# Cached key pages turned on VectorE instead of TensorE, and prompt scores issued one block ahead

## The reference

```python
# prompt, in query blocks of 128 (ci, cum_k: running sums of the log forget values)
s = jnp.einsum('bqhd,bkhd->bhqk', qi, k).astype(jnp.float32) * FOX_SCALE
s = s + jnp.swapaxes(ci, 1, 2)[..., :, None] - cum_k[:, :, None, :]
p = jax.nn.softmax(jnp.where(mask, s, MASK_VALUE), axis=-1)
o = jnp.einsum('bhqk,bkhd->bqhd', p.astype(v.dtype), v)
# samples: pages are taken from a pool by a table
k_past = cache_k[page_table].reshape(DB, P, FOX_HEADS, FOX_DH)
s = jnp.concatenate([jnp.einsum('bqhd,bkhd->bhqk', q, k_past),
                     jnp.einsum('bqhd,bkhd->bhqk', q, k_new)], axis=-1).astype(jnp.float32) * FOX_SCALE
s = s + jnp.swapaxes(cum_new, 1, 2)[..., :, None] - cum_k[:, :, None, :]
p = jax.nn.softmax(jnp.where(mask, s, MASK_VALUE), axis=-1)
o = jnp.einsum('bhqk,bkhd->bqhd', p[..., :P], v_past) + jnp.einsum('bhqk,bkhd->bqhd', p[..., P:], v_new)
```

## Time and profile before

| | us |
|---|---|
| three runs | 2152.65, 2160.13, 2160.87 |
| median | 2160.13 |
| profiled execution, device time | 2150.99 |
| its span | 2149.2 |

### The profile page before, as it was taken

One profiled execution on the slowest core, in us unless ns is written; L12 is line 12 of the kernel. 1 busy time (PEld: TensorE's weight loads), 2 busy tenths in 40 slices (PEclk: granted clock), 3 DMA queues, 4 the chain that ended last, 5 costly groups with the idle time before them and its releaser, 6 DMA issues.

```text
span 2149.2 us, 37580 instructions
## 1 busy us (share of the span) xinstructions
PE 2037.4 (95%) x16263; PEld 1893.7 (88%) x16263; DVE 900.7 (42%) x980; ACT 620.3 (29%) x794; POOL 577.6 (27%) x130
## 2 busy tenths in 40 slices
PE   4999999999889999999999999889998899999998
PEld 3979979979679999999999999666665899999998
DVE  3445245254447424333535325354453562424251
ACT  3222232231235111111233422444444331212121
POOL 1312412503314333333333222000000333333331
PEclk9999999999999999999999999999998899999999
DMA  5142441341423222222321224675763222322221
GB/s 148 63 154 92 138 159 38 128 167 40 142 104 98 79 79 79 78 81 88 100 69 59 79 79 144 228 257 173 246 224 105 93 79 80 96 81 78 78 84 58
DMA packets 169029, 238.87 MB, mean 111 GB/s; under 512 B 12930, under 2 KB 131842, under 8 KB 168706
## 3 DMA queue, kind: packets, MB, share of 16 engines
q1 hardware_dynamic: 151554, 212.61, 30.2%
q10 hardware_dynamic: 17264, 23.79, 3.1%
q0 software_dynamic: 80, 0.52, 0.1%
HBM read 210.77 MB, written 26.12 MB: 110 GB/s over the span
## 4 chain that ended last, share of the span: by engine, by line
PE 65%; issue 23%; DVE 4%; POOL 4%; ACT 2%; DMA 1%; SPq 0%; POOLq 0%; ACTq 0%; DVEq 0%
PE PS L741 15%; PE PS L740 15%; PE PS L742 15%; POOL w_lo L697 4%; PE PS L780 3%; PE PS L781 3%; PE PS L782 3%; PE PS L1167 2%; PE PS L1118 1%; PE PS L1129 1%; PE PS L1155 1%; DVE probs L2099 1%; PE PS L1110 1%; PE PS L1187 1%; PE PS L1228 1%
## 5 line engine op out<-in xcount | busy, mean ns | idle before, releaser
L697 POOL TENSOR_TENSOR w_lo<-w_raw,w_hi 128x2048 fp32r<-128x2048 f32 (+1 forms) x125 | 576.1, 4609 | 1540.4 <-ACT w_hi L1343 1540.4
L1343 ACT ACTIVATE w_hi<-w_raw 128x2048 fp32r<-128x2048 f32 (+1 forms) x125 | 237.9, 1903 | 1028.3 <-PE PS L742 839.6
L740 PE MATMUL PS<-x_hi,w_hi 128*128 128x296 f32 (+1 forms) x1664 | 498.4, 300 | 9.3 <-DVE x_lo L1758 6.1
L741 PE MATMUL PS<-x_lo,w_hi 128*128 128x296 f32 (+1 forms) x1664 | 498.0, 299 | 0.0
L742 PE MATMUL PS<-x_hi,w_lo 128*128 128x296 f32 (+1 forms) x1664 | 497.1, 299 | 0.0
L740 PEld LDWEIGHTS PS<-x_hi,w_hi 128*128 128x128 f32 x1664 | 314.9, 189 | 11.8 <-DVE x_lo L1758 7.5
L741 PEld LDWEIGHTS PS<-x_lo,w_hi 128*128 128x128 f32 x1664 | 314.8, 189 | 0.2
L742 PEld LDWEIGHTS PS<-x_hi,w_lo 128*128 128x128 f32 x1664 | 314.7, 189 | 0.0
L742 PE MATMUL PS<-hidden_hi,w_lo 128*128 128x296 f32 (+1 forms) x1024 | 304.9, 298 | 0.0
L741 PE MATMUL PS<-hidden_lo,w_hi 128*128 128x296 f32 (+1 forms) x1024 | 304.3, 297 | 0.0
L740 PE MATMUL PS<-hidden_hi,w_hi 128*128 128x296 f32 (+1 forms) x1024 | 304.3, 297 | 0.0
(11 more groups left out here) (237 smaller groups left out, 2614.7 us busy)
## 6 DMA issues: line engine op xcount, KB each, us to landing
w_raw<-in_w_mlp_up SPq DMA_DIRECT2D x32, 1024.0 KB, 5.4
w_raw<-in_w_mlp_down SPq DMA_DIRECT2D x32, 1024.0 KB, 5.2
k_page<-in_cache_k SPq DMA_DIRECT2D x64, 512.0 KB, 4.8
v_page<-in_cache_v SPq DMA_DIRECT2D x64, 512.0 KB, 5.4
w_raw<-in_w_ret_in SPq DMA_DIRECT2D x24, 1024.0 KB, 6.1
sample_state<-in_state_ret SPq DMA_DIRECT2D x32, 512.0 KB, 5.4
out_state_ret_sample<-sample_state ACTq DMA_DIRECT2D x32, 512.0 KB, 4.3
w_raw<-in_w_ret_out SPq DMA_DIRECT2D x16, 512.0 KB, 3.4
```

Source lines behind the costliest of these rows:

```text
L697: pool.tensor_tensor(lo, raw, hi.bitcast(F32), ALU.subtract).then_inc(lo_done, 1)
L740: pe.matmul(o, wh[:, w], xh[:, t, cols], start=(t == 0), stop=False)
L741: pe.matmul(o, wh[:, w], xl[:, t, cols], start=False, stop=False)
L1343: act.activation(part(WH[n.slot], n), part(WR[n.slot], n), ACT.Copy).then_inc(hi_done, 1)
```

## The change

- **Key pages.** SP fetches a page in four DMAs, one for each group of four heads, each onto 32 partitions: partition `32a + r` holds rows `r, 32 + r, 64 + r, 96 + r`, of each the 256 floats of heads `4a` to `4a + 3`. DVE turns the page with one transpose instruction, which transposes every 32x32 square within its 32 partitions, into one of four `k_page_t` tiles of eight groups `j`; partitions then hold four heads x 32 dimensions. There are no page turns on PE and no page copies on ACT and DVE any more.
- **Queries.** `q_blocks` is built once for all samples, block diagonal: 32 columns are four heads x 8 queries. The order of heads in sample scores, in `selb` and in the value products follows it.
- **Page scores** are made for two pages at once (`pair_scores`): eight products of 256 columns for a pair.
- **Prompt pairs.** `scores(j)` stands before `probs_t(j - 1)`, in other PSUM banks (3 to 5 for scores, 4 and 6 for turned probabilities, 7 for values); `scores` waits for the exponentials of `j - 1`. The normalising moves from DVE to ACT, and the two reciprocals become one instruction.
- **Metas.** The two heads' probabilities lie side by side in one tile, so the metas of a pair are turned as one 128x32 square, and multiplied by a block-diagonal `meta_v_by_head` in one product.
- **Sample probabilities** are turned into banks 6, 7 and 2; the second half waits for `gated` of the round's slot 0. `out_t` stands first in its slot.
- **Buffers.** Four key and six value buffers; the first two weight blocks of the output projection are loaded at the end of the stage.

The diff, cut to its core:

```diff
-NKS, NVS = 5, 5
+NKS, NVS = 4, 6
+NTURN = 4
...
             def k_page(kn):
+
                 if kn < NPAGE * DB:
-                    page_in(PT1, kn, k_pool, KR, NKS, k_in)
+                    rows = io["cache_k"][page_at(kn)].rearrange("o (i r) (a h) d -> a r (o i) (h d)", r=32, a=4)
+                    for a in range(4):
+                        sp.dma_start(KR[kn % NKS][32 * a:32 * a + 32, :].rearrange("r (i f) -> r i f", i=4), rows[a]) \
+                            .then_inc(k_in[kn % NKS], 16)
...
             for b in range(DB + 1):
...
+                for p in range(4):
+                    k_next(b, p)
+                for p in range(4, 8):
+                    if b == DB and p == 4:
+                        sp.wait_ge(ss_ready, DB)
+                        weights(Blk(N_OUT), w_fo[:, :, 0:BW])
+                    k_next(b, p)
+                    v_next(b - 1, 2 * p - 8)
+                    v_next(b - 1, 2 * p - 7)
+            weights(Blk(N_OUT + 1), w_fo[:, :, BW:2 * BW])
...
                 if j:
-                    pe.wait_ge(pt_evac, 3 * j)
+                    pe.wait_ge(ex_done, 2 * j)
...
                 if j:
                     pe.wait_ge(pv_evac, j)
-                for par in range(2):
-                    src = PP[par][:, m:m + NMETA] if par == 0 else PP[par][:, 0:NMETA]
-                    last = pe.transpose(PS[0:NMETA, 6, 2 * P + P * par:3 * P + P * par], src, ident)
-                last.then_inc(pt_ready, 1)
+                pe.transpose(PS[0:2 * NMETA, 7, 2 * P:3 * P], PP[:, NKEY - NMETA:NKEY + NMETA], ident) \
+                    .then_inc(pt_ready, 1)
...
+            def pair_scores(b, r):
+
+                n = 4 * b + r
+                pe.wait_ge(k_turned, 2 * n + 2)
+                if n == 0:
+                    pe.wait_ge(qb_done, 1)
+                s = 2 * n % NTURN
+                q_k(b, r // 2, slice(2 * P * (r % 2), 2 * P * (r % 2) + 2 * P), lambda j: KP[:, s:s + 2, j, :]) \
+                    .then_inc(sc_used, 1)
...
                 pe.wait_ge(sex_done, b + 1)
...
+                for half, ready in enumerate((sp0_ready, sp1_ready)):
+                    if half:
+                        pe.wait_ge(pv_evac, 4 * b + 3)
                     for p in range(4):
...
+            def slot0(b, j):
+                if b > 1:
+                    out_t(b - 2)
+                if live(j):
+                    scores(j)
+                    probs_t(j - 1)
+                if b > 0:
+                    pair_scores(b - 1, 3)
+                    new_scores(b - 1)
+                if live(j):
+                    values(j - 1)
+
+            def slot1(b, j):
+                if live(j):
+                    probs_t(j - 1)
+                    scores(j)
+                    values(j - 1)
+                if b < DB:
+                    bias(b)
+                if b > 0:
+                    probs_t_s(b - 1)
+                if 0 < b < DB:
+                    pair_scores(b, 0)
...
+            def normed_probs(j):
+                act.wait_ge(inv_row, j + 1)
+                n = keys_of(j % 4)
+                for par in range(2):
+                    x = own_probs(par, n)
+                    act.activation(x, x, ACT.Copy, scale=RM[:, par:par + 1]).then_inc(pn_done, 1)
...
+            def turn_page(kn):
+
+                dve.wait_ge(k_in[kn % NKS], 64 * (kn // NKS + 1))
+                if kn >= NTURN:
+                    dve.wait_ge(sc_used, (kn - NTURN) // 2 + 1)
+                dve.transpose(KP[:, kn % NTURN], KR[kn % NKS][:].rearrange("p (i j c) -> p j i c", i=4, j=8)) \
+                    .then_inc(k_turned, 1)
...
+                    if live(j):
+                        for par in range(2):
+                            maximum(j, par)
+                    if k:
+                        turn_page(NPAGE * b + 2 * i)
+                    if live(j):
+                        inverse_sums(j)
                     if i == 0 and v:
                         maxima_s(b - 1)
+                    if k:
+                        turn_page(NPAGE * b + 2 * i + 1)
+                    if live(j - 1):
+                        gated(j - 1)
                     if i == 1 and v:
                         probs_copy_s(b - 1)
...
+                    if i == 3 and v:
+                        output_s(b - 1)
             gated_s(DB - 1)
```

More of the change, by code:

```diff
@@ L1112, in scores, with query @@
[L1112 to L1121 removed]
+                def query(par):
+                    rows = slice(DH * par, DH * par + DH)
+                    return rows, TQ[rows, 1 + qb, P * t:P * t + P]
@@ new lines, in scores @@
+                if qb == 3:
+                    pe.wait_ge(pt_evac, 3 * j - 2)
+                for par in range(2):
+                    pe.matmul(parts(par)[1], sel(par), CU[:, 0:NMETA], start=(par == 0 and qb == 3), stop=False,
+                              skip_group_check=True)
+                for par in range(2):
+                    rows, q = query(par)
+                    if par == 1 and qb == 3:
+                        pe.wait_ge(s_ready, 2 * j + 1)
+                    pe.matmul(parts(par)[1], q, KTT[rows, t, NSAMP:W0], start=False, stop=True, skip_group_check=True)                         .then_inc(s_ready, 1)
@@ L1306, in _, with slot3 @@
+            def slot3(b, j):
+                if live(j):
+                    scores(j)
+                    probs_t(j - 1)
+                    pair_scores(b, 2)
+                if b > 0:
+                    page_values(b - 1, 4)
+                    page_values(b - 1, 5)
+                if live(j):
+                    values(j - 1)
+                if b > 0:
+                    page_values(b - 1, 6)
+                    page_values(b - 1, 7)
+                    new_values(b - 1)
             pe.wait_ge(rounded, 1)
@@ L1307, in _ @@
             for b in range(DB + 1):
[L1308 to L1317 removed]
+                slot0(b, pair_at(b, 0))
+                slot1(b, pair_at(b, 1))
+                slot2(b, pair_at(b, 2))
@@ L1713, in _ @@
+                    if live(j - 1):
+                        probs_copy(j - 1)
+                    if live(j):
+                        for par in range(2):
+                            exp(j, par)
+                        normed_probs(j)
+                    if i == 0 and b > 0:
+                        exp_s(b - 1)
+                    if i == 1 and b > 0:
+                        probs_copy_s(b - 1)
+            w_hi(Blk(N_OUT))
             act.wait_ge(out_stored, 16 * 6)
```

479 lines of the change are left out of this document (144 added, 335 removed).

## The result

The changed kernel takes 2133.64 us (median of 4 runs, 2128.92 to 2142.42) against 2160.24: a ratio of 0.9885, interval 0.9855 to 0.9916. It is faster, by 27 us where 62 were forecast, and 6 us above the forecast's range. The profiled execution took 2128.92 us (span 2127.1), 22.1 less than that of before.

A forecast was written before the change was run, and what follows sets the result against it. TensorE was taken to set the pace, with short waits beside its work. From 2151.0 profiled, 40.6 us for seven rounds, 7 at the start and 7.5 at the end gave 2095.9; 2 added made 2098 us, range 2064 to 2128.

The forecast's parts named there:

- End: From round nine's first slot 0 scores to the stage's end: 27 us plus about 3 for low clock, gain 7.5.
- transpose: Key page turn on VectorE: 1.23 us each like a plain pass, eight a round, 9.8 us, leaving VectorE under TensorE.
- Start: Stage's start up to slot 0 of round two: gain 7 us, between 3 and 9, after the fifth key page lands.
- Waits: TensorE's waits for other engines through one round: 5.8 us in sum, where 3.0 stood before.
- output's turn: Start of a round, `out_t` first in its slot: TensorE waits 1.5 us for the whole chain after the last value products.
- second sample turn: Slot 1, second half of the sample probabilities: TensorE waits 2.1 us for the next `gated`.
- metas' turn: Third turn in slot 1: TensorE waits 1.5 us for `gated` of the pair before, behind VectorE's other work.
- slot 0: From slot 0 to slot 1: TensorE waits 0.7 us for normalised probabilities it is to turn.
- Slots 2 and 3: Last two slots of a round: short-block chain fits beside TensorE's six to seven us a slot, so no wait.
- Key pages come slowly: Rival: key DMAs onto 32 partitions get half the rate, keys need 23.2 us, a round 34.8, time 2111; chance 0.20.
- The clock: TensorE's fall to 1.2 GHz behind waits: one fall in each round, 0.75 us more than already held.
- Scores and metas: TensorE's work a round: no added cost for prompt pairs' scores; half the metas' turns and products gone, 1.1 us less.

The follow-up runs named there:

- e5: Changed kernel with the first four key ring refills (pages 5 to 8 of sequence 0) issued ahead of the first six value pages on SP; 2140.97 us.
- e8: Changed kernel with each key page fetched in one DMA of 128 partitions x 4 KB, sample scores from misplaced keys; 2112.93 us.
- e13: Changed kernel with each key page fetched in one DMA of 128 partitions, four 1 KB pieces repeating each key's first 256 columns; 2117.03 us.
- e3: Changed kernel plus unread identity products on TensorE, eight ahead of a round's last two value pages, seven ahead of the output's turn; 2130.51 us.
- e10: Changed kernel with each key page in four DMAs of 128 partitions x 256 columns, plain source rows, sample scores from misplaced keys; 2128.24 us.
- e4: Changed kernel with score products of pairs of one to three key blocks grouped again, four of 128 rows, then four of 64; 2131.76 us.
- c8: Changed kernel with value pages on ScalarE's queue, grouped scores, gate's product before slot 1's second page turn, and the fillings of e3; 2116.30 us.
- e1: Changed kernel with each key page in four DMAs of 128 partitions x 256 columns by head group, same layout in the buffer; 2298.62 us.

## Why the prediction was wrong

- **End, transpose: right.** The end took 31.1 us of 30, the turn on VectorE 1.235 us of 1.23. VectorE's group over the rounds:

```profile
L2042 DVE STREAM_TRANSPOSE k_page_t<-k_page 128x1024 f32<-128x1024 f32 x57 | 70.2, 1235 | 0.7 <-DMA k_page<-in_cache_k 0.7
```

  The Trainium skill's figure ("VectorE: DVE Perf Modes", "The three transpose paths") gave an estimated 2.5 us; the measured half of that decides. (By the prediction's own sum, rounds of 36 us would have given 2119 there, not 2115.)
- **Start: the time came by luck, the step was wrong.** Slot 0 of round two stood at 1358.02 where 1359 was forecast, but 6.5 of the 7.7 us are the stage ahead. The start itself gained 1.2 us of 7: TensorE waits 10.5 us there, behind VectorE's 12.6 for the fifth key page. That six value pages stand ahead of it was in the text, as a doubt about the 7; `e5` shows that they were it.
- **Waits: the sum right by luck.** 5.3 us a round of 5.8. The output's turn took 1.5 as forecast, the second sample turn 1.4 of 2.1, the metas' turn 0.7 of 1.5, slot 0 none of 0.7; the 1.6 for value pages, which were not forecast, made up for the rest. So the miss of 4.7 us a round stands in the sum as TensorE's work, 32.4 against 27.05. The prediction's own sign of being wrong, a round over 36 us, was there.
- **The step that failed: "Slots 2 and 3 ... Wait: none."** It looked at TensorE and VectorE alone; that SP and the transfers bring the pages in time was taken for granted. "Key pages come slowly" was a rival with 0.20, and the sum held nothing of it. The rival named the partitions' rate and 2111. With the four narrow DMAs replaced in `e8`, 20.7 us of the 35.6 that were missed go, 3.4 us a round in `e13`: 2.4 of work at a higher clock and 0.9 of waits. The four issues on SP, which the walk left out, seem the larger part; this is argued from the waits and not shown by the times. The place was wrong too: not VectorE at the turn (0.7 us) but TensorE at the value pages behind them. Of the rate itself: if the share is read as time, 25.2 us for 16 wide pages is 1.58 each (332 GB/s), so a narrow one takes 1.58 + 0.76 = 2.34 us, an estimated 224 GB/s. The Trainium skill's 189 for 32 partitions ("SBUF — State Buffer", "Door 1: The DMA port swizzle") has the direction right and is lower than this.
- **The clock, mis-sized.** 0.75 us a round was counted, one short fall. TensorE's work is 32.4 us a round at 0.86 and 30.0 in `e13` at 0.94, the same instructions: 2.4 for that step alone. With the same idle time filled, `e3` comes to 29.9. The rounds' clocks are of one execution each, but over all four executions the clock of the whole span was 0.962 to 0.969 in the changed kernel, 0.972 to 0.978 in `e13` and 0.975 to 0.979 in `e3`. How much idle time there is doesn't tell the clock: 3.9 us a round went with 0.86 in `e10`, 4.3 with 0.94 in `e13`. Which of the waits lower it wasn't separated.
- **Scores and metas, mis-sized.** From start to start at the upper clock (in `e13`, which has the changed order), the four pairs' scores of a round took 1.09 (128 keys), 1.31, 1.62 and 2.09 us before, 6.1 in sum, and take 1.44, 1.71, 2.02 and 2.79 now, 8.0: 1.8 us a round more, which was counted at nothing. The scores of 128 keys before, and what came next:

```profile
1502.31 0.33 PE L1110 MATMUL PS<-cum_parts,negsel_r 128*128 128x128 f32 x1
...
1503.41 0.30 PE L1219 MATMUL PS<-c_keep_sb,sample_probs 128*64 128x128 f32 x1
```

  Grouping by rows gives the first three their old price back, 1.1 us (`e4`, and `c8` for 384 keys, where the clock was up); the scores of 512 keys, which it left alone, stay at 2.79. Metas: a turn takes 1496.14 - 1495.94 = 0.20 and the one product 1498.42 - 1498.00 = 0.42, where two turns took 0.21 and two products 0.36. So the 1.1 us a round that was forecast for them is not there: half the products went, and the ones that stayed got as long as two.
- **The sum.** Work was 5.4 us a round above the forecast: clock 2.4, scores 1.8, metas 1.1 make 5.3.

## What to carry over

When one transfer becomes several, count each issue on its queue with all that is asked for behind it: in a stage where SP is busy for 30 of the 37.7 us of a round, the page that is late is the next one in the queue, not the one that was split. Price idle time of TensorE with the clock behind it: here 5.3 us of waits a round came with some 2.4 more. Price a new order of products by rows of that order, not by how many there are. Measure a stage from its own beginning, since the stages ahead may end some us earlier or later. And a wait removed alone may show nothing, since the next (value pages, then the gate) stands just behind it; three edits that could not be told from nothing one by one gave 22 us together with the value pages on another queue.

## Not expected of the hardware

- Four DMAs with the same bytes and 1 KB pieces took SP 1.85 to 2.21 us to issue onto 32 partitions, 1.9 to 2.5 onto 128 from plain rows (`e10`), and 4.5 onto 128 from a source of three strides (`e1`).
- Products of 128 and of 64 rows in alternation take longer than grouped ones: 1.44 against 1.10 us for the scores of 128 keys.
- A product of 32 rows that replaces two of 16 saved nothing: 0.42 us against 0.36 for the two.
